# A recurrence moved from between projection matmuls to between the products of the next step's triangular inverse

## The reference

```python
p = h @ w_in                                   # 1024 -> 8 blocks of 1024, and three low ranks
cb, cc, ch, ga, gb = ...                       # plain
r, k, v, wd, ad, gd = ...                      # each mixed with the token before
y_conv = cb * causal_dwconv(cc * ch, conv_w)
decay  = exp(-exp(-softplus(-(w0 + tanh(wd) @ decay_up)) - 0.5))
a = sigmoid(a0 + ad @ aaa_up);  g = sigmoid(gd) @ gate_up
kk = k * k_k, normalized by head;  k = k * (1 + (a - 1) * k_a)
def step(state, inp):                          # 16 heads of 64, one token at a time
    sa = einsum('bhvk,bhk->bhv', state, kk_t)
    state = state * w_t - sa[..., None] * (kk_t * a_t) + v_t[..., None] * k_t
    return state, einsum('bhvk,bhk->bhv', state, r_t)
y = norm_by_head(y) * ln_x_w + ln_x_b;  y_rwkv = (y + sum(r * k * r_k) * v) * g
merged = sigmoid(ga) * y_conv + sigmoid(gb) * y_rwkv;  mix = merged @ w_out
```

## Time and profile before

| | |
|---|---|
| median of 3 runs | 5508.87 us (5507.02 to 5515.28) |
| profiled execution, its time | 5513.11 us |
| its span | 5511.2 us |
| its mean granted TensorE clock | 0.957 of full speed |
| PE busy | 5093.8 us (92%) |
| DVE busy | 1764.7 us (32%) |
| ACT busy | 1415.1 us (26%) |
| the mixer's 32 steps | from 285.81 us to 3568 us of the span |

### The profile page before, as it was taken

How to read it: one execution, slowest core, us unless ns; L and a number is a source line. 1 busy time by engine, 2 the same in 40 slices (tenths; PEclk the granted TensorE clock), 3 DMA queues, 4 the chain that set the end, 5 groups by cost and what they waited for, 6 DMA issues and landing times.

```text
span 5511.2 us, 97586 instructions
## 1 busy us (share of the span) xinstructions
PE 5093.8 (92%) x38809; PEld 2682.3 (49%) x38809; DVE 1764.7 (32%) x3775; ACT 1415.1 (26%) x3000; POOL 151.8 (3%) x274
## 2 busy tenths in 40 slices
PE   6699999999999999999999999799599999999970
PEld 1345555555555555555555555445344444444430
DVE  1233434434334334334344343322411111111124
ACT  1613223232232232232232322223111111111115
POOL 0000000000000000000000000000000000000013
PEclk8699999999999999999999999799699999999985
DMA  5110100100100100100100100033488888888865
GB/s 200 65 45 11 41 7 11 41 7 11 41 7 11 41 9 9 41 11 12 37 11 14 34 11 7 35 120 118 155 338 339 329 336 338 338 327 339 337 235 197
DMA packets 252238, 635.90 MB, mean 115 GB/s; under 512 B 10825, under 2 KB 95995, under 8 KB 251902
## 3 DMA queue, kind: packets, MB, share of 16 engines
q1 hardware_dynamic: 238224, 580.70, 29.0%
q0 software_dynamic: 13680, 49.81, 2.6%
HBM read 561.77 MB, written 68.71 MB: 114 GB/s over the span
## 4 chain that ended last, share of the span: by engine, by line
PE 91%; DMA 3%; DVE 3%; ACT 2%; issue 2%; SPq 0%; ACTq 0%; DVEq 0%; POOL 0%; POOLq 0%
PE bank L784 35%; PE bank L1043 16%; PE bank L872 8%; PE bank L1063 8%; PE bank L969 4%; PE bank L865 2%; PE bank L868 2%; PE bank L809 1%; PE bank L818 1%; PE bank L828 1%; PE bank L695 1%; PE bank L1032 1%; PE bank L665 1%; DMA x<-x_s 1%; DMA adaw<-in_w_ada_dram 1%
## 5 line engine op out<-in xcount | busy, mean ns | idle before, releaser
L784 PE MATMUL bank<-hT,w 128*128 (+1 forms) x4096 | 2018.8, 615 | 13.6 <-DMA w<-in_w_in_dram 13.6
L784 PEld LDWEIGHTS bank<-hT,w 128*128 128x128 f32 x4096 | 704.9, 189 | 648.2 <-issue 593.9
L1043 PE MATMUL bank<-WI,xT 128*128 128x512 f32 x2016 | 877.6, 593 | 2.4 <-DVE xT L1830 2.4
L1043 PEld LDWEIGHTS bank<-WI,xT 128*128 128x128 f32 x2016 | 378.8, 190 | 456.1 <-issue 456.1
L1063 PE MATMUL bank<-WO,aT 128*128 128x512 f32 x1008 | 443.1, 592 | 0.7 <-ACT aT L1090 0.7
L1479 DVE SCALAR_TENSOR_TENSOR St<-St,pcs,bank 64x64 f32<-64x64 f32 x512 | 143.3, 280 | 909.5 <-PE bank L830 905.8
L1090 ACT ACT_TABLE_LOAD x291 | 373.4, 1283 | 11.3 <-DVE ub L1587 5.3
L1836 DVE TENSOR_TENSOR gsig<-bank,gsig 128x512 f32<-128x512 f32 x63 | 43.6, 691 | 883.8 <-ACT gsig L1090 883.8
L1063 PEld LDWEIGHTS bank<-WO,aT 128*128 128x128 f32 x1008 | 186.7, 190 | 212.4 <-issue 211.4
L1090 ACT ACTIVATE gsig<-bank 128x512 f32<-128x512 f32 x63 | 37.6, 597 | 821.9 <-PE bank L1043 821.9
L1090 ACT ACTIVATE tok<-bank 128x256 f32<-128x256 f32 x192 | 63.2, 381 | 714.2 <-PE bank L868 714.2
(11 more groups left out here) (308 smaller groups left out, 5023.3 us busy)
## 6 DMA issues: line engine op xcount, KB each, us to landing
WI<-in_w_expert_in_dram SPq DMA_DIRECT2D x63, 4096.0 KB, 17.1
WO<-in_w_expert_out_dram SPq DMA_DIRECT2D x63, 2048.0 KB, 7.9
w<-in_w_in_dram SPq DMA_DIRECT2D x64, 512.0 KB, 4.0
y_s<-ysb SPq DMA_DIRECT2D x63, 512.0 KB, 17.7
adaw<-in_w_ada_dram SPq DMA_DIRECT2D x12, 2048.0 KB, 7.6
xt<-in_x_dram SPq DMA_DIRECT2D x16, 512.0 KB, 3.2
WAc<-rank_s SPq DMA_DIRECT2D x32, 256.0 KB, 3.2
GDc<-rank_s SPq DMA_DIRECT2D x32, 256.0 KB, 3.2
```

Of the source, the lines that this page charges most:

```text
L784: ins = mm(PJ[j % 2][:, :], w[:, j, k, :], hT[:, k, ds(group(i) * G, G)], start=k == 0, stop=k == KT - 1)
L1043: ins = mm(GU[j][:, :], xT[:, s, k, :], WI[:, s, k, j * DE:j * DE + DE], start=k == 0, stop=k == KT - 1)
```

## The change

1. The 24 hops of the recurrence of step i-1 leave the head. They run inside the grams of step i: `sched_plan` puts one hop ahead of the first product and one behind each entry. There are 20 products; LT, GK and Q of level 4 are cut in two entries each (turn 0 and turn 1), which makes 23 entries and 24 hops. The projections run without anything between their matmuls.
2. The order of the products is L, LT, GK, TR0, Z1, T1, Q1, Z2, TR1, T2, Q2, Z3, TR2, T3, Q3, Z4, T4, Q4, Z5, Q5. No projection matmul stands among them; projection 0 opens the head of its own step, ahead of `zdec` and `zaaa`.
3. A recurrence now runs while the next step's operands are made: AR, LTb, GKb, Qm, tok, conv, gg, bv and pcs exist twice, and the loops on all engines take two steps per turn.
4. The banks: x, u and the increment go to PJ[0] and PJ[1], the output to M0 and M1. So the first hop of a step waits for both gates (ACT) and the last of the step's `branch` results (`bv` on DVE), and for `S_init`, which DVE makes behind `bv`; projection 0 of the next step waits for the last `S_update`; `zdec` waits for `copy_y`.
5. DVE and ACT follow the same list: evacuations of an entry's product, then `S_update` or the copies of x and u, in the order of `SCHED`.
6. `centred`, `variance` and `post` come two steps behind instead of one, and the store of the result with them. Behind step 31 those of step 30 stand among the last recurrence's hops (on DVE `post(30)` behind the last `S_update`), in banks SA and SB; `copy_y(31)` waits for `post(30)`.

```diff
+    plan += fill[0:4]
     for lv in range(1, 6):
         plan += [("Z", lv, 0, 0), ("Z", lv, 1, 0)]
-        plan += fill[2 * (lv - 1):2 * lv]
+        if lv in (2, 3):
+            plan += fill[2 * lv:2 * lv + 2]
...
+def sched_plan():
+    hops = [(name, c) for c in range(NC) for name in ("x", "u", "sy")]
+    uses = []
+    for u in PLAN:
+        if u[2] == 1:
+            halves = u[0] in ("LT", "GK") or (u[0], u[1]) == ("Q", 4)
+            uses += [(u[0], u[1], (t,)) for t in range(2)] if halves else [(u[0], u[1], (0, 1))]
+    plan = [("hop",) + hops[0]]
+    for n, u in enumerate(uses):
+        plan += [("use",) + u] + ([("hop",) + hops[n + 1]] if n + 1 < len(hops) else [])
+    return plan
...
-        HEADS = [(slice(0, 64), SA), (slice(64, 128), SB)]
-        Y_HEADS = [(slice(0, 64), SC), (slice(64, 128), SD)]
+        HEADS = [(slice(0, 64), PJ[0]), (slice(64, 128), PJ[1])]
+        Y_HEADS = [(slice(0, 64), M0), (slice(64, 128), M1)]
...
+            def proj(i, j):
+                pe.wait_ge(w_in_sem[j], tile_no(i) * 16 + 16)
+                if j >= 2:
+                    wait_released(j - 2, i)
+                elif not first(i):
+                    wait_released(j + 6, i - 1)
+                    if prior2(i) is not None:
+                        pe.wait_ge(S["S_updated"], (i - 1) * NC)
...
+            def seq_x(q, c, p):
                 if c == 0:
+                    if isinstance(q, int) and q == STEPS - 1:
+                        pe.wait_ge(S["yT_copied"], q)
+                    else:
+                        pe.wait_ge(S["gates"], q * 2 + 4)
+                        pe.wait_ge(S["branch"], q * 3 + 6)
                     pe.wait_ge(S["S_init"], q + 1)
...
+            def product(i, p, kind, lv, turns):
+                if 0 in turns:
+                    reads = [r for b in range(2) for r in operands_of(kind, lv, b)]
+                    reads += [PLAN[n - 4] for n in (use_at[kind, lv, b, 0] for b in range(2)) if n >= 4]
...
+            def inverse_and_recurrence(i, p):
+                q = prior(i)
+                pe.wait_ge(S["operands"], i * 5 + 4)
+                for what, name, *more in SCHED:
+                    if what == "use":
+                        product(i, p, name, *more)
+                    elif q is not None:
+                        {"x": seq_x, "u": seq_u, "sy": seq_sy}[name](q, more[0], 1 - p)
+
+            def head(i):
+                proj(i, 0)
                 zdec(i)
                 zaaa(i)
-                proj(i, 1, q)
+                proj(i, 1)
                 sg_transposes(i)
-                proj(i, 2, q)
+                proj(i, 2)
                 cum(i)
                 norm(i)
-                proj(i, 3, q)
+                proj(i, 3)
                 proj(i, 4)
...
             for c in range(NC):
+                seq_x(STEPS - 1, c, 1)
+                seq_u(STEPS - 1, c, 1)
+                if c == 0:
+                    centred(STEPS - 2, SA)
+                seq_sy(STEPS - 1, c, 1)
+                if c == 1:
+                    variance(STEPS - 2, SB)
+            centred(STEPS - 1, SA)
+            variance(STEPS - 1, SB)
...
+                if q is not None:
+                    start_seq(q)
+                for what, name, *more in SCHED:
+                    if what == "use" and name != "TR" and 1 in more[1]:
+                        for b in range(2):
+                            evacuate((name, more[0], b, 0))
+                    if what == "hop" and name == "sy" and q is not None:
+                        S_update(q, more[0], 1 - p)
```

More of the change, by code:

```diff
@@ L65 @@
 NUSE = len(PLAN)
+def sched_plan():
[9 more added lines that the diff above has]
+    return plan
+SCHED = sched_plan()
+assert sum(x[0] == "hop" for x in SCHED) == 3 * NC
 ON_ACT = [u for u in PLAN if u[0] == "TR"]
@@ L182, in build @@
         Kb = sb(p4, "Kb", [P, NC, HD])
-        tok = sb(p4, "tok", [P, 3, NC, HD])
+        tok = [sb(p4, f"tok{x}", [P, 3, NC, HD]) for x in range(2)]
         T3 = sb(p4, "T3", [P, 3, G + 1])
@@ L206, in build @@
         St = sb(p4, "St", [P, 2, HD])
-        pcs = sb(p4, "pcs", [P, NC])
+        pcs = [sb(p4, f"pcs{x}", [P, NC]) for x in range(2)]
         p4.close()
@@ L928, in tail @@
                 bonus(i)
[L929 removed]
+                inverse_and_recurrence(i, p)
             pe.wait_ge(S["cleared"], 5)
[L932 to L947 removed]
+            head(0)
+            tail(0, 0)
+            head(1)
+            tail(1, 1)
+            head(2)
+            with pe.Fori(1, STEPS // 2 - 1) as h:
+                tail(h * 2, 0)
+                head(h * 2 + 1)
+                tail(h * 2 + 1, 1)
+                head(h * 2 + 2)
+            tail(STEPS - 2, 0)
+            head(STEPS - 1)
+            tail(STEPS - 1, 1)
+            for c in range(NC):
+                seq_x(STEPS - 1, c, 1)
[7 more added lines that the diff above has]
+            variance(STEPS - 1, SB)
+            pe.wait_ge(S["S_updated"], STEPS * NC)
             pe.wait_ge(S["bcast_rows"], 64)
@@ L1235, in step @@
                 fn(rn[:, :], rn[:, :], ACT.Exp, scale=-0.5, bias=epsc[:, 2:3]).then_inc(S["rn_step"], 1)
[L1236 to L1238 removed]
+                act.wait_ge(S["proj_done"], i * 8 + 4)
+                fn(chs[:, :], PJ[1][:, :], ACT.Copy).then_inc(S["ch_copied"], 1)
+                if q2 is not None:
+                    centre(q2)
+                    rstd(q2)
                 act.wait_ge(S["proj_done"], i * 8 + 7)
@@ L1253, in _ @@
-            act.wait_ge(S["cleared"], 5)
-            step(0, None)
-            with act.Fori(1, STEPS) as i:
-                step(i, i - 1)
-            for c in range(NC):
-                seq(STEPS - 1, c)
+                if q2 is not None:
+                    act.wait_ge(S["post_step"], q2 * 4 + 4)
+                fn(gg[p][:, :], PJ[1][:, :], ACT.Sigmoid).then_inc(S["gates"], 1)
+                for what, name, *more in SCHED:
+                    if what == "use" and name == "TR":
+                        for b in range(2):
+                            u = (name, more[0], b, 0)
+                            wait_gram(act, i, u)
+                            fn(tok[p][:, more[0], 4 * b:4 * b + 4, :],
+                               bank(u)[:, 0:4 * HD].rearrange("p (c t) -> p c t", t=HD), ACT.Copy)\
+                                .then_inc(S["tok_copied"], 1)
+                    if what == "hop" and q is not None:
+                        if name == "x":
+                            copy_x(q, more[0])
+                        if name == "u":
+                            copy_u(q, more[0])
@@ new lines, in step @@
+                if q is not None:
+                    copy_y(q)
+            act.wait_ge(S["cleared"], 5)
+            step(0, 0)
+            step(1, 1)
+            with act.Fori(1, STEPS // 2) as h:
+                step(h * 2, 0)
+                step(h * 2 + 1, 1)
+            for c in range(NC):
+                copy_x(STEPS - 1, c)
+                copy_u(STEPS - 1, c)
+                if c == 0:
+                    centre(STEPS - 2, SA)
+                if c == 1:
+                    rstd(STEPS - 2, SB)
```

299 lines of the change are left out of this document (114 added, 185 removed).

## The result

| | before | after |
|---|---|---|
| median | 5507.94 us of 4 runs (5506.94 to 5515.28) | 5476.27 us of 4 runs (5473.01 to 5481.58) |
| profiled execution, its time | 5513.11 us | 5481.58 us |
| its span | 5511.2 us | 5479.3 us |
| its mean granted TensorE clock | 0.957 | 0.954 |

The ratio is 0.9941, with the 95% interval 0.9923 to 0.9958: the changed kernel is 31.7 us faster. 5484 was forecast.

What follows compares the result with a forecast made beforehand. PE's instruction stream was taken to bound each 101.45 us step. Grams of 38.5 plus 61.9 elsewhere gave a period of 100.4; with the ends, -25.4 us from 5508.9 gave 5484 us, range 5456 to 5530.

Steps and rivals of the forecast that it cites:

- the signs by which it said that it would be wrong: Hops not 0.25 to 0.4 us start to start, waits over 8 us a step, or steps with a clock under 1.
- end of bonus to the first hop: Ahead of the grams' first hop: PE waits 1.6 us for bv, then S_init, then its way to PE.
- TR0, then x of chunk 2: TR0 waits 0.3 us for LT's banks; x of chunk 2 waits 0.8 for an S_update queued behind LT and GK.
- T1 / T4 / Q5: Products needing the Z before them, with only a hop between: waits of 0.8, 0.7 and 0.8 us.
- projection 0 (last S_update): Behind the grams, projection 0 waits 0.9 us for the last S_update, queued behind Q5's evacuation.
- all else: The period's part outside the grams, projections without hops up to the end of bonus: 61.9 us.
- Hops and products: PE's work in the grams: products with LT and GK 21.4 us, hops 8 x 1.38 = 11.0, together 32.4.
- Waits: PE waits in the grams that fill hid before: 1.6 + 4.6 = 6.2 us a step.
- hops cost only their pairs: Rival, chance 0.12: hops in the grams lose nothing beyond their pairs; period below 99.8, 5440 to 5465 us.
- the clock falls: Rival, chance 0.1: short waits in the grams halve the clock, 1.5 us each; from 17 falls the gain is gone.
- Longer returns: Rival, chance 0.2: PE starts 0.25 us behind late semaphores, hops keep full price; period 101.3 to 102, 5510 to 5530.
- The ends: Step 0's grams 28.2 us; the last recurrence's first hop 34.0 earlier, 8.6 added behind it; all in all -25.4.

Runs made afterwards that it cites:

- e2_nofill: The kernel before with only projection 0 taken out of the grams into its own head, hops left between projection matmuls: 5644.58 us, ratio 1.0244 to before.
- e1_early: The changed kernel with S_init at the start of DVE's step and the wait for bv moved from the first hop to chunk 0's sy hop: 5421.37 us.
- e5_dve: The changed kernel with S_update of chunk 1 ahead of GK's evacuation in DVE's order, nothing else: 5475.36 us, ratio 0.9939 to before.
- e3_place: The changed kernel with the same hops at other places of the same order of products, nothing else: 5402.51 us, ratio 0.9808 to before.
- e1b_init: The changed kernel with S_init moved from behind bv to the start of DVE's step, waits for gates and bv kept: 5463.03 us, ratio 0.9918 to before.
- e4_all: The changed kernel with e1_early, e3_place and e6_tail together: 5335.58 us, ratio 0.9682 to before.
- e6_tail: The changed kernel with post(30)'s five DVE operations spread behind the S_updates of chunks 3 to 7 of the last recurrence: 5467.02 us, ratio 0.9923 to before.

## Why the prediction came out right, point by point

The mechanism was, in the main, the one forecast: hops among 64x64 products cost nearly only their pairs, projections run clean, and waits for DVE that the fill had hidden take most of it back. The time was 7.7 us below the forecast. That it came so close is in part luck: several of its terms were off and compensate, and three of the signs by which it said that it would be wrong came true. Hops are not 0.25 to 0.4 from start to start (u 0.12, sy 0.58), the waits are over 8 us a step, and there are stretches with a clock under 1. So here is each term. Start to start, medians over steps 1 to 30 of after's trace, beside what was predicted (the period is the mean):

```
                                        predicted   measured
period                                  100.4       100.37
  grams with recurrence                 38.5        38.3
    one product                         0.98        0.93 to 0.95
    half of LT or GK                    0.92        0.88
    hop x / u / sy                      0.38/0.27/0.73   0.25/0.12/0.58
    end of bonus to the first hop       1.6         1.85
    TR0, then x of chunk 2              0.3 + 0.8   0 + 1.47
    T1 / T4 / Q5                        0.8/0.7/0.8 1.11/0.78/1.01
    projection 0 (last S_update)        0.9         1.09
    sy of chunk 6; TR1 and x of 5       0.2; 0.1    0.36; 0.54
  all else                              61.9        62.0
```

- **Hops and products: mis-sized, too dear.** The sum kept the hops' price among projections, 1.38 per chunk, and took only 0.1 us per step off for it. They cost 0.95: the 0.12 per pair that the prediction had worked out from the earlier trace rows was all of it, the rest was the change back to a 128x128 weight. With products of 0.93 to 0.95 the work is about 27.9 us, not 32.3. That was the rival "hops cost only their pairs", and its premise held.
- **Waits: mis-sized, too cheap.** Start to start they are 8.2, not 6.2. (The list of waits counts 6.1 for them, since the modelled end of the matmul ahead covers another 0.2 at each.) All stand at the places that were named, but for the 0.3 at TR0, which reuses a bank that is free earlier; it went into x of chunk 2, right behind. The prediction said that half of what hops gained would turn into longer waits; 2.0 us more of waits stand beside 4.4 less of work, which fits, but no run took this apart.
- **What the sum did not hold.** About 0.7 us per step of pauses for which nothing is shown but "issue" (in the 14 steps with one ahead of u of chunk 7 the wait ahead of Q5 is 0.1 to 0.2 instead of 1.0, so a part of this is counted twice), 0.5 for the clock, and small pauses at the borders of hops, about 1. With these 27.9 + 8.2 + 0.7 + 0.5 + 1 is 38.3, beside 38.3 in the median and 38.4 in the mean. So the 38.5 was hit by errors of opposite sign.
- **Rival "the clock falls": partly true.** It fell where the prediction had looked, behind x of chunk 2 and the T1 behind it, in 7 steps, and in 5 at the first hop, which it had not named; never at projection 0. But it fell in 12 steps, short of the 17 at which the gain would be gone, and cost 1.3 each, not 1.5. What the Trainium skill reports of one kernel ("TensorE: Matmul & The Clock Gate", section "A second HAM failure mode: psum-queue depth-cycling"), that short idles between groups of matmuls made the clock swing, agrees with this trace in 12 of 30 steps.
- **"Longer returns": held in part.** The first hop starts 0.54 behind the end of `S_init`, where 0.4 was taken. T1 and Q5 take 0.2 to 0.3 more. Alone it would have carried the period past 101; the cheaper hops paid for it.
- **The ends.** Step 0's grams took 28.0 (28.2 forecast). From `bonus` of step 0 to that of step 1 it took 88.31 (437.81 less 349.50), where 28.2 + 61.9 = 90.1 was counted: `centred` and `variance`, 1.7, don't exist in step 1. The last recurrence came 36.1 earlier (34.0 forecast) though `w` reached the first projection 1.4 later than before. Behind it 5.6 were added, 8.6 forecast: `post(30)` is there in full (the prediction's terms, 3.4, 2 and 3.4, add up to 8.8), `rstd` makes u of chunk 2 wait 2.5 for `xs` where it otherwise waits 0.6, and `centred` and `variance` fell for the most part into waits for the copies that were there anyway.

e2_nofill, e1_early, e5_dve and e3_place show the causes on the chip: with nothing in the grams to fill such waits they cost 135 us; a wait shortened by its own edit gave about what its row says; and the waits for Zm and `S_update` came from the places of the hops. For x of chunk 2 it was DVE's backlog, for the three Zm the way over DVE and back with only a hop in between (DVE was idle before it, 1.6, 0.3 and 0.6 us in the median ahead of Z of levels 1, 4 and 5); other places for the same hops took both away.

Open: the "issue" pauses, 21 us in after and none before. Of the 40, 14 of up to 1.1 us stand ahead of u of chunk 7, in steps 2, 4 and so on up to 28, so always in the same one of the two steps of a loop turn. The other 26 stand inside a product or a sy hop, as the 0.48 at 1764.48 does. In the four other kernels that keep this order it is the same 14 places; in e3_place, where the hops stand elsewhere, 4 of some 50 stand at that hop. So they aren't that hop's. The trace shows what comes ahead of them: each of the 40 ends 2.2 to 2.9 us behind the start of a packet of the instruction queue (q8), and less than a tenth of all moments lie so far behind one. In the middle step such packets start at 1761.73 and 1775.97, and the pauses end at 1764.48 and 1778.76. They would fit as the cause, but no run changed them, so that isn't shown.

## What to carry to other kernels

Put short matmuls beside others of the same tile size, and count what is lost at each change of size from start to start. When a filler is taken out, list every return time it was hiding, and put the new filler where an answer is out or the engine that answers is behind: here the same hops at other places were worth 74 us, more than twice the change itself. A wait on a semaphore that covers a bank should stand at the first instruction that writes this bank; two hops too early it cost 1.4 us a step (e1b_init less e1_early, 41.7 us over 30).

## What the runs showed of the hardware that was not expected

- A pair of 64x64 matmuls on the two diagonal quarters takes some 0.12 us from start to start in float32 with 64 columns, whether it belongs to a product (8 pairs in 0.93) or a hop (1, 2 and 5 pairs in 0.12, 0.25 and 0.58): between the two next to nothing is lost. From a 128x128 weight to a 64x64 one 0.2 us is, and on the way back 0.15: the u hop took 0.27 to the next projection matmul and 0.12 here.
- The clock fell to half after two waits of 1.2 and 0.9 us with 1.8 us of matmuls between (1753.74 to 1755.56 in the middle step), in 7 of 30 steps, and not in the others, which have the same waits. After one wait of 2.4 us (e2_nofill) it fell in 22 of 31. Why in some steps and not in others isn't shown.
- With all the long waits gone (e4_all, none over 1.1 us in steps 1 to 30) it fell in none of these steps. It fell once in step 0, whose grams have no hops.
- The number of falls differs between executions of the same steps: 12 in the profile of after, 6 in that of e6_tail.
